# A two-layer diffusion step with a routed expert MLP: the last expert pair's rows added by a selection matmul, and weight loads held behind the first rows' fetch

## The reference, cut to what matters

```python
def _post_norm(x, out, gain, bias):
    return _layernorm(DEEPNORM_ALPHA * x + out) * gain + bias
...
    e_w = e_prob / jnp.sum(e_prob, axis=-1, keepdims=True) * g_prob
...
    act = jax.nn.silu(a) * u * combine[..., None].astype(t.dtype)
    y = jnp.einsum('nef,efd->nd', act, w_d)
...
        x = _post_norm(x, g_a * out, ln_gain[i, 0], ln_bias[i, 0])
        h = _modulate(x, sh_f, sc_f)
        moe = _hier_moe(h, w_router_group[i], w_router_expert[i], w_expert_gate[i],
                        w_expert_up[i], w_expert_down[i])
        x = _post_norm(x, g_f * moe, ln_gain[i, 1], ln_bias[i, 1])
```

## Time and profile before

| | us |
|---|---|
| median of 3 runs | 1042.45 (1039.91 to 1043.66) |
| the profiled execution, its own time | 1040.08 |
| its span, first to last instruction | 1038.3 |
| mean granted TensorE clock | 0.910 |
| PE busy | 834.9 (80%) |
| DVE busy | 330.6 (32%) |
| POOL busy | 162.3 (16%) |
| ACT busy | 147.9 (14%) |

### The profile page before, as it was taken

How to read it: one execution, slowest core, us unless ns; L and a number is a source line. 1 busy time by engine, 2 the same in 40 slices (tenths; PEclk the granted TensorE clock), 3 DMA queues, 4 the chain that set the end, 5 groups by cost and what they waited for, 6 DMA issues and landing times.

```text
span 1038.3 us, 12829 instructions
## 1 busy us (share of the span) xinstructions
PE 834.9 (80%) x4937; PEld 436.6 (42%) x4937; DVE 330.6 (32%) x810; ACT 147.9 (14%) x341; POOL 162.3 (16%) x250
## 2 busy tenths in 40 slices
PE   3899999998997989979787828998399879778740
PEld 2556565655484333323232326756333323233310
DVE  3013454554872111111111156347411111110117
ACT  1122222233011010110000021201011101010110
POOL 1032030312102021111111002011111111111000
PEclk9999999999987999998898968998599999898975
DMA  9992654285299888999999798535869999999731
GB/s 339 365 365 100 217 166 158 82 323 204 94 345 417 335 355 352 419 417 419 419 419 413 274 336 319 220 128 230 346 267 419 418 419 420 419 419 418 310 125 68
DMA packets 89901, 318.68 MB, mean 307 GB/s; under 512 B 12776, under 2 KB 25800, under 8 KB 65240
## 3 DMA queue, kind: packets, MB, share of 16 engines
q1 hardware_dynamic: 70016, 274.60, 67.1%
q0 software_dynamic: 12992, 22.15, 6.0%
q10 hardware_dynamic: 6808, 20.79, 5.1%
HBM read 313.75 MB, written 26.80 MB: 328 GB/s over the span
## 4 chain that ended last, share of the span: by engine, by line
PE 51%; DMA 34%; DVE 7%; issue 4%; ACT 2%; POOL 2%; SPq 1%; ACTq 0%; DVEq 0%; POOLq 0%
DMA ring<-in_w_expert_up 18%; PE psum L953 18%; PE psum L835 8%; PE psum L781 7%; PE psum L976 5%; DMA h_hT<-in_w_expert_up 4%; DMA ring<-in_w_ada 4%; PE psum L730 3%; DMA arena<-h_scratch,gidx 3%; DMA h_scratch<-h_hT 2%; PE psum L939 2%; PE psum L807 2%; PE psum L1129 1%; DMA arena<-y_scratch 1%; PE psum L886 1%
## 5 line engine op out<-in xcount | busy, mean ns | idle before, releaser
L953 PE MATMUL psum<-ring,arena 128*64 128x512 f32 x880 | 266.8, 647 | 36.7 <-DMA ring<-in_w_expert_up 24.9
L953 PEld LDWEIGHTS psum<-ring,arena 128*64 128x64 f32 x880 | 87.3, 149 | 171.9 <-issue 168.4
L976 PE MATMUL psum<-ring,arena 128*64 128x512 f32 x440 | 124.1, 598 | 20.1 <-DVE arena L1723 19.4
L953 PE MATMUL psum<-h_hT,arena 128*64 128x512 f32 x208 | 102.0, 648 | 12.9 <-DMA ring<-in_w_expert_up 12.0
L1719 DVE TENSOR_TENSOR arena<-arena,psum 128x256 f32<-128x256 f32 x34 | 14.3, 421 | 305.0 <-ACT arena L1253 305.0
L835 PE MATMUL psum<-ring,h_hT 128*128 128x384 f32 x288 | 98.2, 495 | 0.0
L593 POOL DMA_INDIRECT y_scratch<-arena,sidx x34 | 34.4, 1012 | 241.6 <-DVE arena L1729 235.9
L781 PE MATMUL psum<-ring,h_hT 128*128 128x512 f32 x160 | 69.5, 593 | 1.1 <-ACT h_hT L1338 0.7
L835 PEld LDWEIGHTS psum<-ring,h_hT 128*128 128x128 f32 x288 | 54.4, 194 | 35.1 <-issue 1.8
L730 PE MATMUL psum<-ring,silu 128*32 128x128 f32 x1536 | 53.5, 299 | 16.4 <-DMA ring<-in_w_ada 16.0
L976 PEld LDWEIGHTS psum<-ring,arena 128*64 128x64 f32 x440 | 35.6, 136 | 71.3 <-issue 46.9
(11 more groups left out here) (185 smaller groups left out, 876.2 us busy)
## 6 DMA issues: line engine op xcount, KB each, us to landing
ring<-in_w_expert_gate SPq DMA_DIRECT2D x52, 1024.0 KB, 17.8
ring<-in_w_expert_up SPq DMA_DIRECT2D x52, 1024.0 KB, 24.0
ring<-in_w_expert_down SPq DMA_DIRECT2D x52, 1024.0 KB, 25.9
ring<-in_w_ada SPq DMA_DIRECT2D x24, 2048.0 KB, 14.9
h_hT<-in_w_expert_gate SPq DMA_DIRECT2D x12, 1024.0 KB, 17.1
h_hT<-in_w_expert_up SPq DMA_DIRECT2D x12, 1024.0 KB, 23.2
h_hT<-in_w_expert_down SPq DMA_DIRECT2D x12, 1024.0 KB, 26.6
ring<-in_w_qkv SPq DMA_DIRECT2D x9, 1024.0 KB, 12.4
```

Of the source, the lines that this page charges most:

```text
L953: last = pe.matmul(bank[b][64 * e:64 * e + 64, :].rearrange("p (g n) -> p g n", g=2), mem.GT[b][:, c, 64 * e:64 * e + 64], w, start=(c == ...
L976: last = pe.matmul(bank[5 + half][64 * e:64 * e + 64, :], mem.actT[b][:, f, 64 * e:64 * e + 64], w[:, f, 512 * half:512 * half + 512], sta ...
```

## The change

**Last pair.** The last pair (experts 30 and 31, `LAST`) is no longer scattered. Its `down` result in PSUM is multiplied by the two gates into `gated` (context, latent), and a matmul with a selection matrix `sel` (weights at token and row positions, built from `row_hot`, transposed on PE, copied by ACT) puts it onto each token's row in PSUM. The rows of `y_scratch` are loaded by SP when the scatter of pair 14 has landed. Rows of a token whose expert is in the last pair are never written, so both `y_scratch` tensors are first filled with zeros by SP. If the last pair needs extra passes they run before its ordinary one. In layer 1, x and the earlier pairs' rows are also added in PSUM, by a matmul with the identity (`kept`).

**Order in the last pair.** In layer 0 ACT scales the rows after its SiLU; in layer 1 before it. In layer 1 DVE forms ALPHA x + y of tiles 0 and 1 before its product of the last pair and of tile 2 after it. In layer 0 tile 0 is formed in the last pair and tiles 1 and 2 in `layer_end`.

**Loads.** `first_rows_fetched` puts the loads of experts 2, 3 and 4 (layer 0) and of expert 4 (layer 1) behind both first gathers. Expert 1 of layer 0 is loaded earlier and ada unit (1,3) later. Ada units 6 and 7 of layer 1 are loaded after the rows of `y_scratch` have landed, unit 8 after the sums are read; before, all three were requested when pair 14 was done. Units 9 and 8 change places. The four columns of layer 1 are transposed at the end of routing.

**Semaphores** are merged: `lam_in` with `ctx_in`, `cond_in` with `rows_in`, `h_out` with the zero stores.

```diff
-ADA_ORDER = ... [(1, u) for u in range(ADA_UNITS)]
+ADA_ORDER = ... [(1, u) for u in (*range(8), 9, 8, 10, 11)]
...
+            def first_rows_fetched(l):
+                for b in range(2):
+                    sp.wait_ge(main[l][f"gathered{b}"], 16)
             def load_last_slot(l):
+                first_rows_fetched(l)
...
+            def load_rows(l):
+                sp.wait_ge(main[l]["d_ps"], LAST)
+                sp.wait_ge(main[l]["o_free"], PAIRS + 2)
+                for t in range(TILES):
+                    sp.dma_start(mem.Y[t], y_dram[l].rearrange("(k t p) n -> t p k n", k=2, p=P)[t]
+                                 ).then_inc(y_in[t], 16)
+                if l == 0:
+                    sp.dma_start(mem.dft, A["k_dft"]).then_inc(dft_in, 16)
...
             load_expert(0, 0)
+            sp.wait_ge(zeroed, 5)
+            for l in range(2):
+                sp.dma_start(y_dram[l].rearrange("(c p) n -> p c n", p=P), bc(mem.zero.unsqueeze(1), [P, 2 * TILES, D])
+                             ).then_inc(scratch_out, 16)
             sp.wait_ge(qkv_ps, 24)
             load("ada", 1, 1)
...
-                        for u in (6, 7, 8):
+                        load_rows(0)
+                        for t in range(TILES):
+                            sp.wait_ge(y_in[t], 16)
+                        for u in (6, 7):
                             load("ada", 1, u)
...
+            pool.wait_ge(scratch_out, ZEROED)
             norm_rows(0, 0)
...
-            dve.wait_ge(lam_in, 16 * 5)
+            dve.wait_ge(ctx_in, 16 * 7)
...
                 gt(S, 0, 16, 0)
+                pe.wait_ge(route_out, 3 * l + 3)
                 passes(pe, l, S, first, body)
...
+                    if n == LAST and l == 1:
+                        scale_rows()
                     silu(S, n, b)
...
+                    if n == LAST and l == 1:
+                        keep(l, 0)
+                        keep(l, 1)
                     up_times(S, n, b)
...
+            def gated_evict(S, l):
+                dve.wait_ge(S["d_ps"], PAIRS)
+                for i in range(2):
+                    for half in range(2):
+                        part = slice(512 * half, 512 * half + 512)
+                        V.tensor_tensor(mem.gated[i][:, part], bank[5 + half], mem.gates[:, i, part], ALU.mult
+                                        ).then_inc(kept_gated, 1)
...
+            def output_rows():
+                dve.wait_ge(gb_in, 32 * 4)
+                for t in range(TILES):
+                    asked = ask_root(sum_stats(1, t), t)
+                    times_gain(1, t)
+                    times_root(t, asked).then_inc(x_done, 1)
```

More of the change, by code:

```diff
@@ L61 @@
 PLACE.update({("out", 0, 0): "A0", ("out", 0, 1): "A1"})
-PLACE.update({("ada", 1, u): place for u, place in enumerate(("A2", "C1", "A2", "C1", "A0", "A1"))})
+PLACE.update({("ada", 1, u): place for u, place in enumerate(("A2", "C1", "A2", "A0", "A1", "A2"))})
 PLACE.update({("ada", 1, 6): "A0", ("ada", 1, 7): "A1", ("ada", 1, 8): "A2", ("out", 1, 0): "B0", ("out", 1, 1): "B1",
@@ L215, in __init__ @@
         at[0] += 6 * PASSES * EXPERTS
+        self.pick = [a[:, at[0] + TOK * k:at[0] + TOK * k + TOK].rearrange("p (t e s) -> p t e s", t=TILES, e=2) for k in range(2)]
+        at[0] += 2 * TOK
+        self.first_w = small(2 * TILES)
+        self.pick_w = small(2 * TILES, 2)
         assert at[0] <= 30 * K
@@ L487, in _ @@
                     load("ada", 1, 9)
-                    for u, before in ((10, 6), (11, 7)):
-                        after_ada(1, before)
-                        load("ada", 1, u)
+                    after_ada(1, 6)
+                    load("ada", 1, 10)
+                    sp.wait_ge(sums_read, TILES)
+                    load("ada", 1, 8)
+                    after_ada(1, 7)
+                    load("ada", 1, 11)
                     after_ada(1, 11)
@@ L707, in _ @@
                     pool.wait_ge(m_out, stored[0])
-                for tiles in ([0], [1, 2]):
-                    root(tiles)
-                    if l == 0:
-                        root(tiles)
-                    if l == 0 and tiles == [0]:
+                for n, t in enumerate((0, 0, 1, 2, 1, 2) if l == 0 else range(TILES)):
+                    root([t])
+                    if l == 0 and n == 3:
                         pool.wait_ge(norm_ready, 7)
@@ L1116, in _ @@
             project(1, 0, (0, 1), (1,))
-            for u in (10, 11):
+            for u in (8, 10, 11):
                 ada(1, u)
@@ L1710, in route @@
                         ada_add(1, u)
+                    columns(1)
             def gt_evict(S, n, b):
@@ new lines, in layer_end @@
+            def layer_end():
+                dve.wait_ge(gb_in, 32 * 2)
+                asked = ask_root(sum_stats(0, 0), 0)
+                times_gain(0, 0)
+                link(times_root(0, asked))
+                dve.wait_ge(root_out, ask_root(tile_stats(0), 0))
+                normalised([0])
+                ada_add(1, 6)
+                keep(0, 1)
+                ada_add(1, 7)
+                keep(0, 2)
+                first = [ask_root(tile_stats(t), t) for t in (1, 2)]
+                row_times_gain(1)
+                link(times_root(1, first[0]))
+                second = ask_root(tile_stats(1), 1)
+                row_times_gain(2)
+                times_root(2, first[1]).then_inc(gb_used, 1)
+                dve.wait_ge(gb_used, 2)
+                dve.wait_ge(root_out, second)
+                normalised([1])
+                dve.wait_ge(root_out, ask_root(tile_stats(2), 2))
+                normalised([2])
@@ L1796, in _ @@
             mlp(0)
-            columns(1)
-            for tiles in ([0], [1, 2]):
-                finish_stats(combine(0, tiles), tiles)
-                normalised(tiles)
-                if tiles == [0]:
-                    for u in (6, 7, 8):
-                        ada_add(1, u)
+            layer_end()
             ada_add(1, 9)
@@ L1815, in _ @@
             mlp(1)
-            for tiles in ([0], [1, 2]):
-                combine(1, tiles)
+            output_rows()
 _INS = ["x_prompt", "x_sample", "cache_k", "cache_v", "c", "c_ctx", "w_ada", "b_ada", "ln_gain", "ln_bias", "w_qkv",
```

316 lines of the change are left out of this document (182 added, 134 removed).

## The result

The changed kernel took 1044.09 us (median of 20 runs, 1041.11 to 1051.64) against 1041.14 for the kernel before (20 runs, 1036.77 to 1045.43): ratio 1.0031 [1.0016, 1.0046]. It is slower by 0.3%, with 1.0 outside the interval. 1030.5 was forecast, with 1019 to 1039.5 as the range; 1044.09 lies outside it and on the other side. By the prediction's own limit of 0.3% the result stands on the border between "no change" (chance 0.08) and "slower" (0.09).

The account below looks back on a forecast made before the run. Chain half PE, a third DMA, with weight loads the limit in layer 1's expert phase; +4.1 + 6 - 3 - 3 - 4.9 - 9.4 = -10.2 from 1040.08 gave 1029.9, stated as 1030.5 us; range 1019 to 1039.5.

Parts of the forecast that it names:

- step 3: Layer 0, first rows: held loads let the gather land in about 3.2 us; -3 us, with expert 1's move priced at 0.
- Step 2: Zero stores ahead of ada unit (1,1), where DMA is already full: PE stalls for that unit, +6 us.
- rival D: Zero stores run at under half the rate of loads, PE stalls 21 us instead of 6: 1045.5 us, chance 0.08.
- Rival A: Zeros cost nothing (1 us) and layer 0's earlier norm counts (-7 at its end): 1021 us, chance 0.2.
- Step 1: Merged wait at the start: DVE's lambda work also waits for the cached values, until 61.3; +4.1 us, bounds 3 and 5.5.
- Step 4: Layer 0, end: ada unit (1,9) lands 4.9 us earlier, less 1.9 for unit 8 on PE's path; -3 us.
- Step 5: Layer 1, first rows: with expert 4 held back the gather lands sooner and the first product starts earlier; -4.9 us.
- The forecast's condition: Prediction is wrong if layer 1's expert phase between 761 and 985 us changes length by more than 2 us.
- Rival B: The change doesn't shorten the first-row fetch in either layer, so both gains there are 0: 1038 us, chance 0.1.
- Step 6: Layer 1, end: last pair combined without scatter; down starts 8.3 us later and runs 5.4, yet the end comes -9.4 us.

Follow-up runs that it names:

- the run on the kernel before: Kernel before plus only expert 1 requested ahead of ada unit (1,3), and units 3 to 5 of layer 1 in places A0, A1, A2: ratio 1.0037.
- the kernel with the three out: Changed kernel with lambdas waiting alone, zero stores ahead of ada unit (1,0), and old order and places of ada units 3 to 5 and expert 1: 0.9854.
- the two built like the kernel before: The kernel before itself (1041.14 us), and it with only the changed order and places of expert 1 and layer 1's ada units 3 to 5 (1.0037).
- the three parts: Merged lambda wait, zero stores' place, and ada units 3 to 5 with expert 1's order; undone singly on the changed kernel: 0.9974, 0.9949, 0.9985; together 0.9854.

## Why the prediction was wrong, by its own steps

**The step that failed** is the last sentence of step 3, "Expert 1 was moved earlier, off this place: 0". It priced what the move frees and not what it displaces: expert 1 took place C1, so unit (1,3) went to A0, which is free only at the projections' end, and pushed (1,4) back by its 2.1 MB, 5.2 us at 405 GB/s. The places in the kernel's own table say so, and the section on the change even names unit (1,3) as loaded later; I gave it no price. In the trace it costs 9.8: 6.6 of idle, 1.8 because units 2 to 4 then take 5.43 + 3.64 and not 7.23, and 1.3 because DVE gets the routing products 2.9 after their start (335.32 to 338.20) and not 1.6. Part of it comes back, because the same late units leave DMA empty at the gather, as the run on the kernel before shows; net it is 4.8 in the changed kernel (0.9985 against 1.0031) and 3.9 on the kernel before (1.0037).

**Step 3 itself**, -3: the trace shows -3.8 at the first product, and 1.4 more since it ran in 7.09 instead of 8.49, but not by the mechanism forecast, so the size is luck. The premise "held loads let the gather land in about 3.2" is what failed: without the hold the product starts at the same time (350.90). Where expert 1's load is beside the gather, as in the kernel with the three out, the gather takes 8.66 with the hold, since the hold doesn't cover expert 1. Before the change that load stood there too, issued at 307.18.

**Step 2**, +6: 10.8 in the trace, 8.5 in the runs. The mechanism, the place and the order of waits were right, the size not. I counted 13.6 MB from the first load to unit (1,1). The window at the head of this part moved 386 GB/s for 38.7 us, which is 14.9 MB. Of these 14.3 are on the queue of the weight loads, 0.7 more than counted, which fits the start of unit (1,2), requested at 248, and 0.6 on POOL's queue, where the new cache is stored and rows are loaded. Both shared the DMA and were missing from the sum (3.4 us). The unit behind the stall ran at half clock, 1.7 more. The rate taken, 385, was right, and rival D (stores at half the rate of loads) is excluded by it: the result was slower, but not through slow stores. Rival A (the zeros cost 1) is excluded as well.

**Step 1**, +4.1: 5.8 in the trace, 5.9 in the runs. The wait is as computed (61.3 forecast, 62.82 with a start 1.4 later); the rest is PE at half clock after it, the upper bound of 5.5 and a little.

**Step 4**, -3: -2.8. Unit (1,9) lands 4.5 earlier when the 19.5 of delay is taken off (4.9 forecast), unit 8 on PE's path costs 1.8 (1.9 forecast), and the rows' gain stayed off the path: tile 0 is normalised from 627.50, 10.7 earlier than before by the same count. Rival A's half on this is excluded.

**Step 5**, -4.9: -5.3, and the runs without the hold lose it (8.35 for the gather, 6.5 us in the medians). The forecast's condition held too: the DMA-bound phase has the same 224 us at 405 GB/s. Rival B is excluded. The Trainium skill's DMA: Bandwidth & Descriptors, in its section on queues, rings and completion order, has each DMA engine alternate between queues packet by packet. An even share of the bytes, as I read that rule, would make the gather some 1.5 us slower beside a backlog (an estimate: 0.52 MB at 379 GB/s and at half of it); it takes 8.4 us beside one of 3 MiB and 3.4 alone, so the trace decides against that reading. How many bytes of each queue go in one turn, no run here shows.

**Step 6**, -9.4: -9.2, and that it is so close is luck. `down` was held back by 7.8 (8.3 forecast), and it ran in 3.65 and not 5.4. Between the idle time and `down` stand the matmuls of `kept` (3.58 for four, where four such take 1.98 at full clock), which the prediction left out; the granted clock is 0.69 from 1010 to 1014.5 and 1.00 after. The Trainium skill's TensorE: Matmul & The Clock Gate, Part 1, gives an idle PE its full clock back only after sustained work. The trace agrees: the work was `kept`'s, and `down` came behind it. DVE ends at 1033.35, 0.7 earlier than before, although pair 14's eviction was 11.4 later: 12.0 gained. Then 2.8 are lost. From DVE's last operation to the end of the span it takes 7.1, where the sum carries over 4.3 from before. In all twelve traces of the changed kernel and of its variants it is 7.1 to 7.2, and in the two built like the kernel before 4.3, so this belongs to the change. The last store is issued at 1033.38, and these stores land in 2.6; what fills the rest stays open.

**The sum.** The forecast missed by 13.6 us. Of this the three parts hold 18.4 against 10.1 forecast: 8.3. The layer 0 hold, forecast at -3, gives 0: 3 more. Of the remaining 2.3, 0.5 is that the median before (1041.14) lies 1.1 above the execution that the sum starts from, for which 0.6 was added; the rest is not assigned. The steps of layer 0's end and of layer 1 are within 0.4 of their sizes in one trace, and an interval of the medians reaches 2 to 4 us to each side. The trace gives the same picture: +2.2 instead of -10.2 is 12.4 off, of which 9.8 is the displaced load, 4.8 step 2, 1.7 step 1 and 1.4 the start, and 4.5 is given back in layer 0's expert phase, for which no step stood; the other steps are off by -0.8 together. The chance of 0.09 for slower was too low since all rivals of that sign were one: nothing stood for a moved load whose place isn't free.

## What to carry to other kernels

When a load is moved, write down not only its own new time but which buffer it takes, who had that buffer, and at which event the displaced load's new buffer is free; then price the displaced load from that event. Ask of each stall, removed or added, whether DMA is idle ahead of it: an idle queue before a wait for weights is an order to mend, and filling one can make the transfers behind it collide again. Count into a full stretch what all queues move, not only the one that is changed.

## What the runs showed of the hardware

- A gather of 128 rows of 4 KB, issued by POOL, lands in 3.4 us with DMA free (3.42, 4.34 with little beside it) and took 7.3 to 10.7 on the chains where a backlog of SP's weight loads was there.
- Stores of zeros from one SBUF tile to DRAM run at the rate of loads: the stretch with 6.3 MB of them moved 386 GB/s, its later part (240 to 257) 403.
- A wait on PE of 5 to 10 us costs about 1.7 us more than itself in the work behind it: 3.64 for 64 matmuls that take 1.96, at a granted clock of half.
